# RMSNorm factors applied behind the projections, a router in token rows, and unread products during routing

## The chip, the cores and the metric

The program runs on one core of a Trainium2 chip. The metric is the device time in microseconds (us) of one execution. TensorE is called PE in the rows, VectorE DVE, ScalarE ACT, GpSimd POOL and SyncE SP (SP only issues DMAs here).

## The reference, cut to what matters

Two residual layers over 256 tokens of width 1024, all in float32:

```python
# layer 0
u = rmsnorm(h, ev_norm_mix) @ ev_w_in          # 1024 -> 1952
h = h + attention_a_and_b(u) @ ev_w_out
h = h + swiglu(rmsnorm(h, ev_norm_ff), gate, up, down)          # width 2752
# layer 1
qkv = rmsnorm(h, od_norm_mix) @ od_w_qkv       # 1024 -> 3072
h = h + diff_attention(qkv) @ od_w_out
n = rmsnorm(h, od_norm_ff)
h = h + moe(n, top 2 of 8 by n @ od_router)    # each expert a swiglu of width 3584
```

rmsnorm(x, g) is x * rsqrt(mean(x*x) + eps) * g, by token row. The queries, keys and head outputs have norms of their own, which the change leaves alone.

## The kernel before

**Weights.** They come in units of up to 1 MB (2048 columns on 128 partitions): 66 units for the dense stages, then 42 for each of the 8 experts. SP issues each load into one of RAW = 7 buffers `raw` (four of them in the first stages). ACT rounds a unit to fp32r (`w_hi`, lines 611 and 824), DVE subtracts for the rest (`w_lo`, lines 947 and 1322), and each product of float32 operands is three fp32r matmuls (`product`, lines 1533 to 1535). There are SPLIT = 3 buffers of `w_hi` and `w_lo`, so unit n+3 can be split only when TensorE has used unit n (`unit_used`). Semaphores `hi_ready`, `lo_ready` and `unit_used` count the units. Every engine runs its own program in the order written; a wait holds all that is behind it on that engine.

**Norms.** There are four, k = 0 to 3: ahead of the first input projection, of the dense SwiGLU, of the q/k/v projection, and of router and experts. TensorE accumulates the last unit ahead of norms 1 to 3 in four PSUM banks; when the whole unit is done DVE adds the banks to `h` (`add_out`, line 1052), ACT squares and sums each token half and takes the root (`norm_roots`, lines 642 and 643), DVE takes the reciprocal and multiplies `h` by it into `xs` (`norm_apply`, lines 969 and 970), TensorE transposes `xs` in 16 blocks (`norm_turn`, line 1541), DVE multiplies by the gain (`scale`, line 954), ACT rounds (`parts`, line 618), DVE subtracts (`low_part`, line 961). The next products want the high and low parts of one quarter at a time (`xT_ready`).

**Start.** SP issues the two halves of x, seven gain DMAs, the first weight unit, ten more gain DMAs (`head_gains`), then further units. ACT issues nine small row DMAs (`load_rows`) behind its third split; DVE waits for them, builds eight bias tables (line 1103), and only then splits unit 3. The output of the first 512 columns is copied, squared and normed by DVE and ACT (lines 1107 to 1114), and TensorE turns it (line 1572) behind the second 512 columns.

**Routing.** Logits come as 24 fp32r matmuls with experts as rows, are copied and turned back by TensorE, and DVE picks the two best in 12 dependent steps (lines 1349 to 1363). TensorE counts ranks with five float32 products (lines 1791 to 1795), DVE makes selection matrices `sel` (line 1412), TensorE gathers tokens with them in four groups of eight matmuls (`gather`, line 1806), and ACT and DVE copy the results out of PSUM (lines 899 and 1481). Then DVE lists the overflow work (`spare_items`, lines 1381 to 1406) and expert 0 begins. Gathered rows come from `xn`, the normed rows, split into `xg_hi` (line 893) and `xg_lo` (line 1336).

## Time and profile before

| what | value |
|---|---|
| time, median of 3 runs | 1520.2 us (1518.89 to 1520.89) |
| time of the profiled execution | 1518.86 us |
| its span, first to last instruction | 1516.7 us |
| busy share of the span: PE, DVE, ACT | 95%, 79%, 63% |
| mean granted TensorE clock | 0.966 |

The profiled execution has 2.2 us around its span, and lies 1.3 us below the median. "Idle before <- X" in a row is the time that the engine stood still ahead of the instruction, and X is what let it go. A matmul record is longer than its spacing (0.39 us against a start every 0.23 us), since matmuls are pipelined: the spacing counts.

### The profile page before, as it was taken

How to read it: one execution, taken by the hardware profiler on the slowest of the kernel's cores; microseconds unless marked ns; L12 is line 12 of the kernel's file. 1: busy time of each engine (PE TensorE's matmuls, PEld its weight loads, DVE VectorE, ACT ScalarE, POOL GpSimd, SP SyncE). 2: the span in 40 equal slices, each digit the busy share in tenths (PEclk: the TensorE clock that was granted, in tenths of full speed). 3: DMA queues.
4: the chain of work that ended last, by engine and by line, in shares of the span. 5: the costliest groups of instructions: out<-in, count | busy, mean ns of one | idle time of the engine just before them, and what ended most of it. 6: DMA issues, size and time to landing. Idle time of an engine off the chain costs nothing.

```text
span 1516.7 us, 17820 instructions
## 1 busy us (share of the span) xinstructions
PE 1438.9 (95%) x6619; PEld 1189.3 (78%) x6619; DVE 1191.1 (79%) x1022; ACT 958.9 (63%) x837; POOL 8.4 (1%) x49
## 2 busy tenths in 40 slices
PE   6989899998987699999999999999999999999997
PEld 5768788886866578888888888888888888888886
DVE  7873545445686688899889889888889888888986
ACT  5462534434464367777777777777777777777774
POOL 2000000000000000000000000000000000000000
PEclk9977999999977799999999999999999999999999
DMA  8401755364512269999999999999999998999992
GB/s 278 142 28 51 268 183 192 125 213 142 193 57 85 96 244 375 376 346 375 379 319 377 371 365 359 378 336 344 377 371 347 377 377 311 380 370 354 368 378 112
DMA packets 181295, 421.52 MB, mean 278 GB/s; under 512 B 9192, under 2 KB 12316, under 8 KB 181212
## 3 DMA queue, kind: packets, MB, share of 16 engines
q1 hardware_dynamic: 178172, 418.56, 77.0%
q0 software_dynamic: 560, 1.59, 0.3%
q8 instruction: 57, 0.93, 0.2%
q10 hardware_dynamic: 2480, 0.22, 0.1%
q14 instruction: 26, 0.21, 0.0%
HBM read 419.28 MB, written 1.06 MB: 277 GB/s over the span
## 4 chain that ended last, share of the span: by engine, by line
PE 86%; DVE 9%; ACT 2%; issue 2%; DMA 0%; SPq 0%; DVEq 0%; ACTq 0%
PE ps L1533 26%; PE ps L1535 26%; PE ps L1534 26%; PE ps L1839 2%; DVE w_lo L947 2%; DVE w_lo L1322 1%; PE ps L1806 1%; ACT w_hi L611 1%; DVE h L1434 1%; DVE work L1027 1%; PE ps L1596 1%; PE ps L1541 1%; PE ps L1816 0%; PE ps L1589 0%; PE ps L1612 0%
## 5 line engine op out<-in xcount | busy, mean ns | idle before, releaser
L1322 DVE TENSOR_TENSOR w_lo<-raw,w_hi 128x2048 fp32r<-128x2048 f32 x336 | 768.8, 2290 | 110.3 <-ACT w_hi L824 109.4
L824 ACT ACTIVATE w_hi<-raw 128x2048 fp32r<-128x2048 f32 x336 | 644.2, 1919 | 244.0 <-PE ps L1535 244.0
L1533 PE MATMUL ps<-w_hi,xT_hi 128*128 128x512 f32 (+2 forms) x1312 | 516.5, 394 | 9.4 <-issue 5.3
L1535 PE MATMUL ps<-w_hi,xT_lo 128*128 128x512 f32 (+2 forms) x1312 | 509.0, 388 | 0.0
L1534 PE MATMUL ps<-w_lo,xT_hi 128*128 128x512 f32 (+2 forms) x1312 | 508.7, 388 | 0.0
L1533 PEld LDWEIGHTS ps<-w_hi,xT_hi 128*128 128x128 f32 x1312 | 248.0, 189 | 61.4 <-issue 9.6
L1535 PEld LDWEIGHTS ps<-w_hi,xT_lo 128*128 128x128 f32 x1312 | 247.9, 189 | 51.3
L1534 PEld LDWEIGHTS ps<-w_lo,xT_hi 128*128 128x128 f32 x1312 | 248.4, 189 | 47.8
L947 DVE TENSOR_TENSOR w_lo<-raw,w_hi 128x2048 fp32r<-128x2048 f32 (+4 forms) x66 | 140.6, 2141 | 113.4 <-ACT w_hi L611 113.2
L1533 PE MATMUL ps<-w_hi,hT_hi 128*128 128x512 f32 (+1 forms) x548 | 214.7, 392 | 3.0 <-DVE hT_lo L961 2.0
L1535 PE MATMUL ps<-w_hi,hT_lo 128*128 128x512 f32 (+1 forms) x548 | 213.8, 390 | 0.0
L1534 PE MATMUL ps<-w_lo,hT_hi 128*128 128x512 f32 (+1 forms) x548 | 213.5, 390 | 0.0
L611 ACT ACTIVATE w_hi<-raw 128x2048 fp32r<-128x2048 f32 (+4 forms) x66 | 117.5, 1793 | 135.4 <-PE ps L1535 134.9
L1533 PEld LDWEIGHTS ps<-w_hi,hT_hi 128*128 128x128 f32 (+1 forms) x548 | 103.5, 189 | 24.5 <-DVE hT_lo L961 2.2
L1535 PEld LDWEIGHTS ps<-w_hi,hT_lo 128*128 128x128 f32 (+1 forms) x548 | 103.3, 189 | 21.6
L1534 PEld LDWEIGHTS ps<-w_lo,hT_hi 128*128 128x128 f32 (+1 forms) x548 | 103.4, 189 | 20.7
L849 ACT ACTIVATE hT_hi<-ps 128x512 fp32r<-128x512 f32 x56 | 33.1, 592 | 9.8 <-PE ps L1839 9.8
L1440 DVE TENSOR_TENSOR hT_lo<-ps,hT_hi 128x512 fp32r<-128x512 f32 x56 | 38.3, 684 | 1.3 <-ACT hT_hi L849 1.3
L1456 DVE TENSOR_TENSOR prod_e<-sil_e,ps 128x512 f32<-128x512 f32 x56 | 38.1, 680 | 0.0
L1839 PEld LDWEIGHTS ps<-ident,prod_e 128*128 128x128 f32 x224 | 27.1, 139 | 11.7 <-DVE h L1434 2.9
L1839 PE MATMUL ps<-ident,prod_e 128*128 128x128 f32 x224 | 33.8, 273 | 2.5 <-DVE h L1434 2.5
L874 ACT ACTIVATE sil_e<-ps 128x512 f32<-128x512 f32 x56 | 32.3, 577 | 0.0
(254 smaller groups left out, 739.8 us busy)
## 6 DMA issues: line engine op xcount, KB each, us to landing
raw<-in_od_ex_gate_dram SPq DMA_DIRECT2D x112, 1024.0 KB, 5.8
raw<-in_od_ex_up_dram SPq DMA_DIRECT2D x112, 1024.0 KB, 6.0
raw<-in_od_ex_down_dram SPq DMA_DIRECT2D x112, 1024.0 KB, 5.7
raw<-in_od_w_qkv_dram SPq DMA_DIRECT2D x12, 1024.0 KB, 5.3
raw<-in_ev_ff_gate_dram SPq DMA_DIRECT2D x10, 1024.0 KB, 5.3
raw<-in_ev_ff_up_dram SPq DMA_DIRECT2D x10, 1024.0 KB, 5.3
raw<-in_ev_ff_down_dram SPq DMA_DIRECT2D x10, 1024.0 KB, 4.9
raw<-in_ev_w_in_dram SPq DMA_DIRECT2D x6, 1024.0 KB, 5.6
```

The costliest lines, as they stand in the source:

```text
L611: ins = act.activation(w_hi[0:r, n % SPLIT, a:a + m], raw[0:r, raw_of(n), a:a + m], ACT.Copy)
L824: act.activation(w_hi[:, (DENSE + q) % SPLIT, :], raw[:, r, :], ACT.Copy).then_inc(hi_ready, 1)
L849: act.activation(hT_hi[:, :, side(m)], blocks(4 + m % 2), ACT.Copy).then_inc(hT_part, 1)
L874: act.activation(sil_e[:, j % 2, :], ps[:, 2 * (j % 2), :], ACT.Silu).then_inc(silu_done, 1)
L947: ins = dve.tensor_tensor(w_lo[0:r, n % SPLIT, a:a + m], raw[0:r, raw_of(n), a:a + m], w_hi[0:r, n % SPLIT, a:a + m].bitcast(F32), ALU.sub ...
L1322: dve.tensor_tensor(w_lo[:, k, :], raw[:, raw_of(DENSE + q), :], w_hi[:, k, :].bitcast(F32), ALU.subtract).then_inc(lo_ready, 1)
L1440: dve.tensor_tensor(hT_lo[:, :, side(m)], blocks(4 + m % 2), hT_hi[:, :, side(m)].bitcast(F32), ALU.subtract).then_inc(hT_ready, 1)
L1456: dve.tensor_tensor(prod_e[:, j % 2, :], sil_e[:, j % 2, :], ps[:, 2 * (j % 2) + 1, :], ALU.mult).then_inc(prod_done, 1)
L1533: pe.matmul(out, x_hi, hi, start=start, stop=False)
L1534: pe.matmul(out, x_hi, lo, start=False, stop=False)
L1535: return pe.matmul(out, x_lo, hi, start=False, stop=stop)
L1839: ins = pe.transpose(ps[:, 4 + j % 2, n * P:(n + 1) * P], prod_e[:, j % 2, n * P:(n + 1) * P], ident[:, :])
```

## The change

- **Norm factors.** `h` itself is transposed and multiplied by the gain; the factor 1/rms is applied per token row to what comes out: in the copy of the projections out of PSUM, in the Silu and in the product with it (`rstd` as a per-partition scale). `norm_turn`, `scale`, `parts` and `low_part` no longer wait for roots.
- **Quarters.** `last_unit` orders the last unit by quarters of h (token half, column half), signals each by `out_psum`, and puts the transposes of quarter 0 ahead of the products of the last quarter. DVE adds each quarter by itself (`add_quarter`, `add_and_norm`).
- **Start.** The first two weight units are asked for right behind x; all gain DMAs but one follow them, that one is issued by ACT. Unit 0 is split in halves. DVE's angle steps (lines 1063 to 1080) and ACT's squares come behind the split of unit 1, `load_rows` stays behind the split of unit 2, and `turn_gains` (formerly ahead of the first product) and `router_g` come ahead of the bias tables.
- **Router.** 16 float32 products with tokens as rows, from unnormed `h` and a router multiplied by the gain (the choice of a row does not depend on its factor). No copy and turn of logits; a top search has one step less. Ranks are four products. `xg_hi` and `xg_lo` are made from `hg` = h * gain with the factor in them. `low_tokens(0)` comes ahead of the ranks, `low_tokens(1)` behind `sel`; the split of expert unit 2 and the gate arithmetic (`gates`) move behind the gathered copies, ahead of `spare_items`.
- **Unread products.** `keep_busy` issues 5 fp32r matmuls of 512 columns behind the router and 3 behind the ranks, into a bank that nobody reads.
- **Expert pairs** wait for the first half of the gathered tokens at their first unit and for the second half at their second.

The core of the diff ("..." for what is left out):

```diff
+            def other_gains():
...
-                if n == 1:
-                    head_gains()
+                if n == 2:
+                    other_gains()
...
+            act.wait_ge(gain_ones, 1)
+            act.dma_start(gain_rows[G_MIX0:G_MIX0 + DC, :], w["ev_norm_mix"][0].rearrange("(k p) -> k p", p=P)).then_inc(mix_landed, 16)
...
+                    if n == 0:
+                        act.activation(w_hi[:, 0, 0:UNIT // 2], raw[:, 0, 0:UNIT // 2], ACT.Copy).then_inc(first_hi, 1)
+                        act.activation(w_hi[:, 0, UNIT // 2:UNIT], raw[:, 0, UNIT // 2:UNIT], ACT.Copy).then_inc(hi_ready, 1)
+                        continue
...
+            def norm_square(k, t):
+                if k == 0:
+                    act.wait_ge(x_landed[t], 16)
+                else:
+                    act.wait_ge(h_ready, 4 * (k - 1) + 3 + t)
+                act.activation(squares_3[t] if k == 3 else xs[:, t, :], h[:, t, :], ACT.Square,
+                               accum_out=ssq[:, 2 * k + t:2 * k + t + 1]).then_inc(act_chain, 1)
+                chain[0] += 1
...
+                act.wait_ge(act_chain, chain[0])
+                act.activation(root[:, 2 * k:2 * k + TT], ssq[:, 2 * k:2 * k + TT], ACT.Sqrt,
+                               scale=1.0 / D, bias=eps[:, 0:1]).then_inc(root_ready, 1)
...
+            load_root_table()
+            norm_part(0, 0)
+            split_to(1)
+            for f in range(1, 4):
+                norm_part(0, f)
+            split_to(2)
+            for t in range(TT):
+                norm_square(0, t)
             norm_roots(0)
...
+            def copy_turned(f):
+                t, half = quarter(f)
+                act.wait_ge(xT_psum, 12 + f + 1)
+                act.activation(hT[:, 4 * half:4 * half + 4, t * P:(t + 1) * P], blocks(f), ACT.Copy).then_inc(hT_copied, 1)
+            copy_turned(0)
+            norm_square(3, 0)
+            for f in range(1, 4):
+                copy_turned(f)
+            norm_square(3, 1)
             norm_roots(3)
+            act.wait_ge(rstd_ready, 4)
+            for t in range(TT):
+                act.wait_ge(hg_ready, t + 1)
+                act.activation(xg_hi[:, t, :], hg[:, t, :], ACT.Copy, scale=rstd[:, 6 + t:7 + t]).then_inc(xg_hi_ready, 1)
             split_unit(0, SPLIT - 1)
-            norm_parts(3, 14)
-            for t in range(TT):
-                act.wait_ge(xn_ready, t + 1)
-                act.activation(xg_hi[:, t, :], xn[:, t, :], ACT.Copy).then_inc(xg_hi_ready, 1)
-            act.wait_ge(gate_diff, 1)
-            act.activation(gate_s[:, 5, :], gate_s[:, 4, :], ACT.Exp).then_inc(gate_exp, 1)
...
+            act.wait_ge(gate_diff, 1)
+            for t in range(TT):
+                ins = act.activation(gate_s[:, 5, t:t + 1], gate_s[:, 4, t:t + 1], ACT.Exp, scale=rstd[:, 6 + t:7 + t])
+            ins.then_inc(gate_exp, 1)
...
+            def add_and_norm(stage, last, k, first, c):
+                for f in range(3):
+                    add_quarter(stage, f, last)
+                norm_scale(k, first, c, 0)
+                add_quarter(stage, 3, last)
+                norm_low(c, 0)
+                norm_scale(k, first, c, 1)
+                norm_scale(k, first, c, 2)
+                norm_low(c, 1)
+                norm_scale(k, first, c, 3)
+                norm_low(c, 2)
+                norm_low(c, 3)
+                norm_reciprocals(k)
...
+            norm_scale(0, G_MIX0, 0, 0)
+            norm_scale(0, G_MIX0, 0, 1)
+            norm_low(0, 0)
+            split_to(1)
+            norm_low(0, 1)
+            norm_scale(0, G_MIX0, 0, 2)
+            norm_scale(0, G_MIX0, 0, 3)
+            norm_low(0, 2)
+            norm_low(0, 3)
+            split_to(2)
...
-            dve.wait_ge(router_split, 1)
-            dve.tensor_tensor(router_lo[:, :, :], router[:, :, :], router_hi[:, :, :].bitcast(F32), ALU.subtract).then_inc(router_split, 1)
+            turn_gains()
+            dve.wait_ge(gains_ready, 2)
+            dve.tensor_tensor(router_g[:, :, :], router[:, :, :], gains(G_FF1, DC, E), ALU.mult).then_inc(router_ready, 1)
...
+                dve.tensor_tensor(hg[:, t, :], h[:, t, :], gain_ff[:, :], ALU.mult).then_inc(hg_ready, 1)
+            norm_reciprocals(3)
+            dve.wait_ge(hg_ready, TT)
+            dve.wait_ge(rstd_ready, 4)
...
+            raw_logits = ps[:, 4:6, 0:E]
+            dve.tensor_copy(g[:, 0, :, :], raw_logits)
             def top(src, m, key, hot):
-                link(dve.tensor_reduce(gs[:, m, :], g[:, src, :, :], AX.X, ALU.max))
-                link(dve.tensor_tensor(g[:, key, :, :], g[:, src, :, :], per_token(gs[:, m, :]), ALU.is_equal))
-                link(dve.tensor_tensor(g[:, key, :, :], g[:, key, :, :], keys, ALU.mult))
+                link(dve.tensor_reduce(gs[:, m, :], src, AX.X, ALU.max))
+                for t in range(TT):
+                    ins = dve.scalar_tensor_tensor(out=g[:, key, t, :], in0=src[:, t, :], scalar=gs[:, m, t:t + 1], in1=load8[:, 8, :],
+                                                   op0=ALU.is_equal, op1=ALU.mult)
+                link(ins)
...
+            low_tokens(0)
...
             select(0, 0)
             select(1, 1).then_inc(sel_ready, 1)
+            low_tokens(1)
             for half in range(2):
                 dve.wait_ge(gather_psum, 2 * half + 2)
                 bank = FIRST_BANK[2 * half + 1]
                 dve.tensor_copy(xT_lo[:, 4 * half:4 * half + 4, :],
                                 ps[:, bank:bank + 2, :].rearrange("p b (c n) -> p (b c) n", n=T)).then_inc(x_lo_ready, 1)
+            split_unit(0, SPLIT - 1)
+            gates()
+            dve.wait_ge(rank_psum, 2)
             spare_items()
             dve.wait_ge(routed, 1)
...
+            def last_unit(stage, k, rows, x_hi, x_lo, hi, lo, stop):
+                for f in range(4):
+                    t, half = quarter(f)
+                    tok, col = slice(t * P, (t + 1) * P), slice(half * N, (half + 1) * N)
+                    for c, r in enumerate(rows):
+                        ins = product(ps[:, 4 + TT * t + half, :], x_hi[0:r, c, tok], x_lo[0:r, c, tok], hi[0:r, c, col], lo[0:r, c, col],
+                                      False, c == len(rows) - 1)
+                    ins.then_inc(out_psum if f < 3 else unit_used, 1)
+                    if f == 2:
+                        norm_turn(k, 0)
+                for f in range(1, 4):
+                    norm_turn(k, f)
...
+            def keep_busy(count):
+                for n in range(count):
+                    pe.matmul(ps[:, 0, :], xT_hi[:, n % DC, 0:P], xT_hi[:, 0:2, :].rearrange("p c n -> p (c n)"), start=True, stop=True)
+            pe.wait_ge(router_ready, 1)
+            for f in range(4):
+                t, half = quarter(f)
+                pe.wait_ge(hT_copied, f + 1)
+                for c in range(4 * half, 4 * half + 4):
+                    ins = pe.matmul(ps[:, 4 + t, 0:E], hT[:, c, t * P:(t + 1) * P], router_g[:, c, :], start=(c == 0), stop=(c == DC - 1))
             ins.then_inc(logits_psum, 1)
...
+            keep_busy(5)
             pe.wait_ge(chosen_ready, 1)
...
+            pe.matmul(ps[:, 6, 0:TT * E], tri[:, :], chosen.rearrange("p t e -> p (t e)"), start=True, stop=False)
+            pe.matmul(ps[:, 6, E:2 * E], ones[:, :], chosen[:, 0, :], start=False, stop=True).then_inc(rank_psum, 1)
+            pe.matmul(ps[:, 7, 0:E], ones[:, :], chosen[:, 0, :], start=True, stop=False)
+            pe.matmul(ps[:, 7, 0:E], ones[:, :], chosen[:, 1, :], start=False, stop=True).then_inc(rank_psum, 1)
+            keep_busy(3)
```

## Rows read from the trace of the kernel before

**Rows 1.** The page: the chain that ended last, by engine

```profile
PE 86%; DVE 9%; ACT 2%; issue 2%; DMA 0%; SPq 0%; DVEq 0%; ACTq 0%
```

**Rows 2.** Timeline of all engines, 0 to 42 us (start, length, instruction)

```profile
4.05 0.41 SPq L512 DMA_DIRECT2D raw<-in_ev_w_in_dram  x1
...
9.51 1.91 ACT L611 ACTIVATE w_hi<-raw 128x2048 fp32r<-128x2048 f32 x1 [0.50 <-DMA raw<-in_ev_w_in_dram]
...
16.25 0.77 PE L1533 MATMUL ps<-w_hi,xT_hi 128*128 128x512 f32 x1 [0.78 <-DVE xT_lo L961]
```

**Rows 3.** Busy time in two stretches (last columns: clock, share of 16 DMA engines, GB/s)

```profile
4.00:4.50 0.50, 0.00 (x0) 0.00 (x0) 0.00 (x0) 0.00 (x0) 0.00 (x0) 1.00 0.70 186
...
8.00:8.50 0.50, 0.00 (x0) 0.00 (x0) 0.43 (x3) 0.50 (x1) 0.00 (x0) 1.00 1.03 394
```

**Rows 4.** Timeline of ACT, then DVE, behind the first products

```profile
18.34 0.36 ACTq L595 DMA_DIRECT2D ga_rot<-in_ev_a_qnorm_dram  x1
...
25.84 0.36 DVE L1094 TENSOR_TENSOR lamv<-lamv 128x64 f32<-128x64 f32 x2 [0.56 <-DMA router<-in_od_router_dram]
...
29.54 3.96 DVE L947 TENSOR_TENSOR w_lo<-raw,w_hi 128x2048 fp32r<-128x2048 f32 x2
...
40.38 1.02 DVE L954 TENSOR_TENSOR work<-ps,gcol 128x384 f32<-128x384 f32 x2 [1.78 <-PE ps L1572]
```

**Rows 5.** Timeline of DVE, then PE, around norm 1

```profile
156.67 2.48 DVE L1052 TENSOR_TENSOR h<-h,ps 128x512 f32<-128x512 f32 x4 [1.14 <-PE ps L1535]
...
164.02 0.47 PE L1533 MATMUL ps<-w_hi,xT_hi 128*128 128x512 f32 x1 [0.20 <-DVE xT_lo L961]
```

**Rows 6.** Instructions of one shape, all of them (count | busy us, mean ns)

```profile
L961 DVE TENSOR_TENSOR xT_lo<-work,xT_hi 128x512 fp32r<-128x512 f32 x16 | 11.0, 687 | 1.0 <-ACT xT_hi L618 0.8
```

**Rows 7.** Timeline of DVE, then PE, around norm 2

```profile
355.11 2.48 DVE L1052 TENSOR_TENSOR h<-h,ps 128x512 f32<-128x512 f32 x4 [0.26 <-PE ps L1535]
...
362.54 0.77 PE L1533 MATMUL ps<-w_hi,xT_hi 128*128 128x512 f32 x1
...
364.76 0.39 PE L1535 MATMUL ps<-w_hi,xT_lo 128*128 128x512 f32 x1
```

**Rows 8.** Timeline of DVE, then PE, norm 3 and routing

```profile
501.12 2.48 DVE L1052 TENSOR_TENSOR h<-h,ps 128x512 f32<-128x512 f32 x4 [1.14 <-PE ps L1535]
...
519.99 0.17 DVE L1349 COPY gate_t<-ps 128x16 f32<-128x16 f32 x1 [0.47 <-PE ps L1786]
...
522.48 0.17 DVE L1363 TENSOR_TENSOR gate_t<-gate_t 128x16 f32<-128x16 f32 x1
...
525.32 0.88 DVE L1412 TENSOR_SCALAR sel<-slots_f,rank 128x128 fp32r<-128x128 f32 x4
...
483.82 0.93 PE L1624 MATMUL ps<-ident,xs 128*128 128x128 f32 x7
...
524.43 0.57 PE L1795 MATMUL ps<-gate_t,ones 128*128 128x8 f32 x2
526.25 2.08 PE L1806 MATMUL ps<-sel,xg_hi 128*128 128x256 f32 x8 [1.24 <-DVE sel L1412]
...
534.20 0.47 PE L1533 MATMUL ps<-w_hi,xT_hi 128*128 128x512 f32 x1 [1.36 <-issue]
```

**Rows 9.** Timeline of DVE, then ACT, first units of expert 0

```profile
532.87 1.22 DVE L1481 CAST xT_lo<-ps 128x1024 fp32r<-128x1024 f32 x1 [1.58 <-PE ps L1806]
534.01 0.15 DVE L1381 TENSOR_SCALAR load<-ps 128x8 f32<-128x8 f32 x1
...
539.32 2.29 DVE L1322 TENSOR_TENSOR w_lo<-raw,w_hi 128x2048 fp32r<-128x2048 f32 x1 [0.46 <-ACT w_hi L824]
...
540.02 1.92 ACT L824 ACTIVATE w_hi<-raw 128x2048 fp32r<-128x2048 f32 x1 [0.80 <-PE ps L1535]
```

**Rows 10.** Busy time and granted clock (third column from the end) in stretches

```profile
44.00:45.00 1.00, 1.00 (x5) 0.85 (x4) 0.42 (x2) 1.00 (x2) 0.00 (x0) 0.50 0.00 0
...
98.50:132.00 33.50, 32.04 (x129) 27.06 (x129) 15.63 (x40) 14.15 (x42) 0.00 (x0) 0.50 0.10 32
```

267 lines of the change are left out of this document (139 added, 128 removed).

## Prediction

> **What bounds the kernel now.** I read the page's chain first: TensorE holds 86% of it, DVE 9%, ACT 2% [rows 1]. So the chain is TensorE's products, and what can be won or lost lies where it leaves TensorE. Its pieces in order of time leave TensorE at the start (first product at 16.25), at the four norms, in both attentions, and in routing. The attentions are untouched and only shift. I then read a timeline of each engine at each changed place. All times are in the profiled execution (1518.86 us); it lies 1.3 below the median, and I add that at the end. T below is the time at which DVE's additions to h begin, which is when the last unit's results are there.
>
> **Start.** The first unit is asked for at 4.05 and is there at 9.5; then 1.9 for its rounding, 2.3 for its subtraction, and norm work, until 16.25 [rows 2]. Asked for at about 1.8, it has only x ahead of it. At 8 us the DMA engines are full at 394 GB/s [rows 3]; x and this unit are 2.1 MB, or 5.3 us at that rate from about 3, so I take 8.4 for the landing (8 to 9.4). Halving lets rounding and subtraction overlap: 1.0 + 1.2 + 1.2 gives 11.9, which is the first product, 4.3 earlier.
>
> Most of this is not kept. Behind the split of unit 1 (DVE until 18.8) come ACT's squares and root, then ACT's nine row DMAs. ACT: split of unit 1 until 16.5, two squares 2.3, so that its row DMAs start at 19.05 in place of 18.34, and the rows land at 26.5 in place of 25.8 [rows 4]. DVE cannot pass that wait. Behind it stand 0.75 of lambda work, 0.65 of `turn_gains` and router product (0.2 before), the bias tables of 2.8, and the splits of units 3 and 4 of 3.96 [rows 4]; all end 1.15 later than before. Unit 3 is ready at 33.0, while TensorE wants it at 30.9. TensorE then waits again for the normed columns (39.4). Before, DVE waited 1.8 us for TensorE at that place [rows 4]; now TensorE waits for DVE. The chain goes on at 39.9 in place of 40.4: **0.5 us won**. Bounds: 4.3 if DVE holds nothing up, -1.0 if the unit lands at 9.4 and everything behind it shifts.
>
> The engines' share was 0.70 at 4 us, with 186 GB/s [rows 3]; that is the gap which I expect the early request to fill, and the bound of 9.4 is for the case that it doesn't. One rule speaks against the new order: the Trainium skill, "Trainium Kernel Development and Optimization", section Key Constraints, says that DMAs issued from several engines share the same 16 engines, so that spreading them saves only issue time. By that rule the early request gives nothing, and the result would be that of rival B. The trace agrees for the time around 8, not for that around 4.
>
> **Norm 1.** T = 156.67, first product of the next stage 7.35 later [rows 5]. DVE stands idle for 1.14 before T, behind a split that stays where it is, so its quarters are added at T-1.14, -0.52 and +0.10, 0.62 each (four in 2.48 [rows 5]), although TensorE had them up to 4 us earlier. TensorE has the transposes of quarter 0 ahead of its last six products: it waits from T-1.56 to T-0.45, turns four blocks warm at 0.11 (0.93 for seven with the tail [rows 8]), and ends the last quarter at T+1.4. DVE: gain on quarter 0 until +1.4, fourth addition until +2.2, ACT's rounding meanwhile, subtraction (0.69) until +2.9 [rows 6]. The other transposes end at +2.7. First product at +2.95: **4.4 won**. The second quarter is ready at about +4.6 and wanted at +5.7; the third at 7, wanted at 8.4. ACT's squares and roots lie beside the products; the factor is wanted by the Silu only 11 us later. That they cost nothing rests on these 11 us.
>
> **Norm 2.** DVE is idle only 0.26 before T = 355.11, so all is 0.8 later: first product at T+3.75 in place of +7.43. Here the clock was also low at the first products: the sixth began 2.22 after the first, where 1.14 is the full-clock pace [rows 7]. TensorE now never idles over 2 us there, so I give that 1.1 back: **4.8 won**. For each norm the low bound is 2.5 (roots or DVE hold the quarters up once more), the high one 5.
>
> **Norm 3 and routing.** T = 501.12 [rows 8]. As for norm 1, the last transposes end at T+2.7. ACT copies the four turned quarters and squares between them; they are there in time. The router is 16 float32 products; a float32 product of 8 columns is two records, 0.21 each at the low clock (five products, ten records, from 522.71 to 524.86 [rows 8]), 0.11 at the full one: 3.5 to 6.9 us. I take 4.0: ends at +6.7, in place of +14.4. Choice: 12 steps took 2.66 from the copy at 519.99 [rows 8]; one fewer with three cheap unlinked ones, 2.3: +9.0. Then 0.35 and `low_tokens(0)` 1.25, which now stands ahead of the rank addition, 0.2, and the selection 0.88 [rows 8]: +11.7. TensorE has three unread products behind the ranks; at the low clock these run to +12.0. The gather took 6.8 us for 32 matmuls, all at the low clock until its end [rows 8]. At the full clock it takes 3.5, at the low one 6.8.
>
> **The clock.** TensorE idled from 40.35 to 42.68, and at 44 it is at half (1.2 GHz), although it works again [rows 10]; during routing it was at half from 518 to 532. In the new order it still idles for 1 to 2 us between router, choice, ranks and gather. Eight unread products are 1.8 us of work at full clock. I do not think that this is enough: it falls during router or choice and rises some 4.6 us after the gather has begun (it rose 3.7 us after the first product at 16.25, and 5.8 us after the gather had begun at 526.25). So gather at half until +16.6, the rest at full: first expert product at +17.7 = 518.8 in place of 534.2: **15.4 won** (18.0 if the clock stays full, 14.2 if it stays low through the gather).
>
> **First units of expert 0.** Before, `spare_items` began at 534.01, 0.2 before the first product, and DVE had the split of unit 3 done at 541.6, while TensorE wanted it at 542.7 (unit 1 done at 540.0, 2.7 a unit) [rows 9]. Now the expert begins when the first half has been copied. With E for its first product DVE has: second copy until E+1.3, split of unit 2 2.3 (moved here), gates 1.15 (moved here), `spare_items` 4.85 (534.01 to 538.86), split of unit 3 2.3: E+11.9. TensorE wants it at E+8.5: **a stall of 3.4**. Idling so long, TensorE falls to half, for about 4 us of products: **2.0 lost** (0 to 3.4). Behind it DVE has two units in hand at once and keeps up (2.29 a unit against 2.72).
>
> Other edits at nothing: factor in copies and Silu (same passes over the same tile), the three-operand product (0.06 more on 12 tiles, not waited for), waits of the later expert pairs (no idle there in the waits view), ranks by four products instead of five.
>
> **Sum:** 0.5 + 4.4 + 4.8 + 15.4 - 3.4 - 2.0 = 19.7. 1518.86 - 19.7 = 1499.2; with the 1.3 to the median, 1500.5.
>
> **Rivals.**
> A. The whole start is kept: 3.8 more, 1496.7. For it: DVE's chain may get its rows earlier. Against: rows wait behind ACT's squares. 0.10.
> B. The first unit lands no earlier: 1.5 less, 1502. For it: full DMA engines. 0.12.
> C. The unread products do keep the clock full, in routing and over the stall: 2.6 + 2.0 more, 1495.9. For it: the idle stretches get much shorter than the 3.7 us ahead of the turned logits. Against: 2.3 us of idling at 40.35 was enough for a fall. 0.13.
> D. The quarters are worth half: DVE is late at each norm, and transposes and products of the last unit wait for it: 2.2 less at each of three, 1507. 0.10.
> E. DVE stays behind in expert 0 and a second stall of some 3.4 follows: 1504. For it: DVE is the second busiest engine there. Against: 0.4 us of slack in each unit. 0.10.
> F. Slower: the clock, once down at the stall, stays down. It has done so from 98.5 to 132 with TensorE busy nearly throughout [rows 10]. A product at half takes 0.43 in place of 0.23, so each us of it loses 0.47, and it decides from 42 us on; 60 us would lose 28, for 1529. Against: at each dense stage it rose within 6 us of the first product. 0.03.
> G. No change, because losses elsewhere just cancel the gain: 0.02.
> The forecast has the remaining 0.40, in a range of its own of 1496 to 1505.
>
> A measurement of this kernel tells 0.2%, or 3 us, from no change. Faster: 0.40 + 0.10 + 0.12 + 0.13 + 0.10 + 0.10 = 0.95; same 0.02; slower 0.03. The range of 1493 to 1507.5 leaves out F, G, half of D and some of C with A together (1492).
>
> **What would show it.** First product near 11.9 but the compressed columns turned near 39.9; next-stage products 3 to 4 us after the last unit at norms 1 and 2, and a wait of TensorE of 1 to 2 us for the first addition inside that unit; the choice done near T+9; the gather at about T+12 with a clock of 0.5; first expert product near T+17.7; a wait of TensorE for the split of unit 3 of 3.4 us, its clock at half behind it. The prediction is wrong if DVE's chain at the start takes another way, if the clock stays at 1.0 through routing, or if that wait is missing.

## The result, and the profile after

The changed kernel takes 1507.77 us (median of 7 runs, 1499.01 to 1512.36) against 1520.89 us before; the ratio is 0.9914, 95% interval 0.9889 to 0.9938. That is 13.1 us faster, where 19.7 us were forecast, and 0.3 us above the upper end of the range. The profiled execution lies at the median: span 1505.7 us against 1516.7, so 11.0 us of gain have to be placed. What strikes first is the spread: 13 us in the runs after, under 3 us in the seven before (in the later calls the kernel before spread by 6 to 9 us as well).

The page's chain still belongs to TensorE [rows 1]:

```profile
PE 84%; DVE 10%; ACT 3%; issue 2%; DMA 1%; ACTq 0%; SPq 0%; DVEq 0%
```

Start, timeline of ACT, PE and DVE (answers to [rows 2, 4]):

```profile
10.69 1.06 ACT L621 ACTIVATE w_hi<-raw 128x1024 fp32r<-128x1024 f32 x1 [1.18 <-DMA raw<-in_ev_w_in_dram]
...
14.24 0.77 PE L1628 MATMUL ps<-w_hi,xT_hi 128*128 128x512 f32 x1 [5.29 <-DVE w_lo L999]
...
20.53 0.36 ACTq L607 DMA_DIRECT2D ga_rot<-in_ev_a_qnorm_dram  x1
...
27.70 0.36 DVE L1180 TENSOR_TENSOR lamv<-lamv 128x64 f32<-128x64 f32 x2 [1.62 <-DMA router<-in_od_router_dram]
...
40.63 1.01 DVE L1011 TENSOR_TENSOR work<-ps,gcol 128x384 f32<-128x384 f32 x2
```

The first unit landed later than before (10.7, not 9.5), though it was asked for 2.3 us earlier; from there to the first product it took 3.5 us, as forecast. Behind DVE's chain of rows, tables and splits nothing is left: 40.63 against 40.38.

Norm 1, timeline of DVE and PE (answers to [rows 5]):

```profile
156.57 1.87 DVE L1049 TENSOR_TENSOR h<-h,ps 128x512 f32<-128x512 f32 x3
157.31 0.66 PE L1641 MATMUL ps<-ident,h 128*128 128x128 f32 x4 [0.91 <-DVE h L1049]
...
160.82 0.47 PE L1628 MATMUL ps<-w_hi,xT_hi 128*128 128x512 f32 x1
```

Norm 2, the same (answers to [rows 7]); the first four rows are the end of the feed-forward stage and its last unit:

```profile
344.92 0.41 PE L1856 MATMUL ps<-ident,work 128*128 128x128 f32 x2 [1.13 <-DVE hT_lo L1313]
...
346.37 0.50 PE L1628 MATMUL ps<-w_hi,hT_hi 128*128 128x512 f32 x1 [1.04 <-DVE hT_lo L1313]
...
348.17 0.72 PE L1628 MATMUL ps<-w_hi,hT_hi 128*128 128x512 f32 x1
...
349.68 0.79 PE L1628 MATMUL ps<-w_hi,hT_hi 64*128 64x512 f32 x1
...
358.31 2.82 PE L1641 MATMUL ps<-ident,h 128*128 128x128 f32 x12
...
360.78 0.78 PE L1628 MATMUL ps<-w_hi,xT_hi 128*128 128x512 f32 x1
```

Here the reader is to see the durations: products of 0.63 to 0.79 in place of 0.39 to 0.50, twelve transposes in 2.82 in place of 1.60. The clock was at half from about 348.2 on, 2 us into the last unit, until 362. The busy time by stretch says the same (last three columns: granted clock, share of the DMA engines, GB/s), and shows the first attention at half from 88 us, where before it was 98 us [rows 10]:

```profile
88.00:98.00 10.00, 8.80 (x37) 0.54 0.01 2
98.00:134.00 36.00, 35.33 (x141) 0.51 0.09 30
...
342.00:348.00 6.00, 3.83 (x17) 1.00 0.00 0
348.00:360.00 12.00, 12.00 (x32) 0.51 0.50 175
```

Routing and expert 0 (answers to [rows 8, 9]):

```profile
501.55 3.64 PE L1913 MATMUL ps<-router_g,xs 128*128 128x8 f32 x32
...
507.63 0.18 DVE L1451 TENSOR_TENSOR gate_t<-gate_t 128x16 f32<-128x16 f32 x1
...
511.02 1.91 PE L1934 MATMUL ps<-sel,xg_hi 128*128 128x256 f32 x8
...
516.83 0.40 PE L1628 MATMUL ps<-w_hi,xT_hi 128*128 128x512 f32 x1
...
528.70 0.50 PE L1628 MATMUL ps<-w_hi,xT_hi 128*128 128x512 f32 x1 [3.52 <-DVE w_lo L1404]
```

I divide the span at instructions which both kernels have: the first products behind norms 1, 2 and 3 (the rows above and [rows 5, 7, 8]) and the first output of expert 0, whose place is in the view of the tile `y_lo` (first and last start in us), before and after:

```profile
L1427 DVE TENSOR_TENSOR y_lo<-ps,y_hi x16: 678/682/692, 654.3 to 1507.8; 128x512 fp32r<-128x512 f32 x16
```

```profile
L1518 DVE TENSOR_TENSOR y_lo<-ps,y_hi x16: 679/682/692, 642.3 to 1496.0; 128x512 fp32r<-128x512 f32 x16
```

| us won in the stretch | forecast | profile after | the same kernel again (e1_again) |
|---|---|---|---|
| to the first product behind norm 1 | 0.5 + 4.4 = 4.9 | 164.02 - 160.82 = 3.2 | 4.7 |
| to that behind norm 2 | 4.8 | 1.76 - 3.2 = -1.4 | 2.9 |
| to the first expert product | 15.4 | 17.37 - 1.76 = 15.6 | 19.1 |
| to the first output of expert 0 | -3.4 - 2.0 = -5.4 | 12.0 - 17.4 = -5.4 | -6.3 |
| to the end | 0 | 11.0 - 12.0 = -1.0 | -0.2 |
| sum | 19.7 | 11.0 | 20.2 |

The row of norm 2 needs care: 1.1 of its 4.8 us was to be won behind the first product, by the clock, so that the stretch itself was forecast at 3.7 and the next one at 16.5. A narrower distance shows each place better: from the first product of the last unit ahead of a norm to the first product of the next stage. Before and after it is 13.0 and 8.7 us at norm 1, 13.4 and 14.4 at norm 2, 38.7 and 23.7 at norm 3 with routing.

So norm 1 (4.3), routing (15.0 of 15.4) and the stall are as forecast. Norm 2 is not: it lost 1.0 where 3.7 were forecast. Besides, 1.6 us are missing ahead of norm 1, 0.5 between norms 1 and 2, 0.5 between norms 2 and 3, and 1.0 at the end.

### The profile page after: what moved, and what is told of

It reads as the page before. It is cut to its first block, busy times and chain, and to the rows that moved or that the text cites. A ratio compares the mean times of both kernels' runs of the same rounds, so it can differ in the third digit from the quotient of the medians.

```text
span 1505.7 us, 17825 instructions
## 1 busy us (share of the span) xinstructions
PE 1444.6 (96%) x6632; PEld 1190.9 (79%) x6632; DVE 1180.2 (78%) x1003; ACT 957.8 (64%) x833; POOL 8.4 (1%) x49
## 4 chain that ended last, share of the span: by engine, by line
PE 84%; DVE 10%; ACT 3%; issue 2%; DMA 1%; ACTq 0%; SPq 0%; DVEq 0%
PE ps L1628 25%; PE ps L1630 25%; PE ps L1629 25%; DVE w_lo L1004 2%; PE ps L1967 2%; DVE w_lo L1404 2%; PE ps L1934 1%; DVE h L1525 1%; ACT w_hi L627 1%; PE ps L1711 1%; PE ps L1704 1%; DMA raw<-in_ev_w_in_dram 1%; DVE work L1110 1%; PE ps L1703 1%; PE ps L1641 1%
## 5 line engine op out<-in xcount | busy, mean ns | idle before, releaser
L1630 PEld LDWEIGHTS ps<-w_hi,hT_lo 128*128 128x128 f32 (+1 forms) x548 | 103.7, 189 | 21.9
L1711 PE MATMUL ps<-ident,work 128*128 128x128 f32 x72 | 19.6, 404 | 14.5 <-DVE work L1364 11.4
```

What stands on the lines that cost most here:

```text
L1630: return pe.matmul(out, x_lo, hi, start=False, stop=stop)
L1711: ins = pe.transpose(ps[:, 2 + head % 2, n * P:(n + 1) * P], s[:, slot, n * P:(n + 1) * P], ident[:, :])
```

## Experiments

**The same kernel again, and unread work before norm 2.** Theory: nothing in the order is wrong, but TensorE's clock falls in stretches of which the forecast said that they only shift. Rival: the order of the quarters itself costs time. The first run has no edit; in the second, TensorE has unread products where it waited for DVE twice 1.1 us:

```diff
                             ins.then_inc(ff_turned, 1)
+                            if j == FCH:
+                                for n in range(4):
+                                    pe.matmul(ps[:, (4 * (FCH - 1) + 2) % 3, :], xT_hi[:, n, 0:P], ..., start=True, stop=True)
```

> The changed kernel once more, unaltered. Its own profile gained 4.4 us less than forecast at the second norm (clock at half from 348 us, through the last unit of the feed-forward stage and the transposes) and lost 2.4 us in the first attention (half from 88.7 us in place of 98.5). Theory 1: these are falls of TensorE's clock that strike or miss a place from one execution to the next, because work ahead of them leaves TensorE idle for parts of some us; then the times spread again over some 10 us, the median lies at 1505 to 1510, and this profile shows the fall at another place, or none at the second norm (its first product then 2 to 4 us earlier relative to the additions). Theory 2: the order of instructions causes the loss; then the first product of the next stage comes 8 to 9 us behind the first addition again, with the clock low at the same place, and the times agree within 3 us.

> Eight unread products, four behind each of the last two pairs of transposes of the feed-forward stage, where TensorE waited 1.1 us twice (344.0 and 345.3). They take 0.9 us each time and lie inside the wait. Theory 1 (the clock falls at 348 because of these waits): clock full through the last unit and the transposes of norm 2; 24 products at 0.23 in place of 0.43 and four groups of transposes: 4.5 to 6 us faster than the changed kernel where it had the fall, so a median of 1502 to 1505, and a narrower spread. Theory 2 (the order of the quarters costs it): no change in the distance from the first addition to the next stage's first product, median as the changed kernel within 2 us.

Measured, e1_again: median 1504.38 (1488.61 to 1511.16), profiled execution 1498.59, span 1496.5. Its first products and the same stretches:

```profile
159.36 0.47 PE L1628 MATMUL ps<-w_hi,xT_hi 128*128 128x512 f32 x1
...
344.87 0.50 PE L1628 MATMUL ps<-w_hi,hT_hi 128*128 128x512 f32 x1 [1.04 <-DVE hT_lo L1313]
...
354.99 0.47 PE L1628 MATMUL ps<-w_hi,xT_hi 128*128 128x512 f32 x1
...
507.52 0.40 PE L1628 MATMUL ps<-w_hi,xT_hi 128*128 128x512 f32 x1
```

```profile
88.00:98.00 10.00, 7.74 (x58) 1.00 0.01 2
98.00:134.00 36.00, 34.54 (x137) 0.50 0.09 30
...
342.00:348.00 6.00, 3.84 (x16) 1.00 0.00 0
348.00:360.00 12.00, 11.01 (x53) 1.00 0.50 175
```

The instructions are the same. The last unit began 1.5 us earlier here, so I compare the 6 us ahead of it: TensorE was busy for 3.84 us from 338.87 to 344.87 here and for 3.83 us from 340.37 to 346.37 in the profile after. The clock then stayed at 1.00 here and fell to half there. Behind the fall in the attention TensorE sets the pace, 3.58 us a head:

```profile
98.44 0.79 PE L1703 MATMUL ps<-raw 64*128 64x128 f32 x2
...
102.02 0.79 PE L1703 MATMUL ps<-raw 64*128 64x128 f32 x2
```

From the first product of the last feed-forward unit to the first of the next stage it took 10.1 us here, 14.4 in the profile after, 13.4 before (349.09 to 362.54). Every profile of this order with full clock at that place agrees with the 10.1 (e2_fill, e10 and e15 below). This execution gained 20.2 us. That it is so near 19.7 is partly luck: norm 2 with full clock gave less than forecast, while the stretch behind it gave 19.1 in place of 16.5, with the clock at half for 23.5 us in the second attention (30.5 before) and back earlier in the gather. So theory 1 holds, and the 13 runs of the two calls say how wide it is: 1488.6 to 1512.4 us, mean granted clocks 0.980 to 0.960, about 1.2 us for each 0.001.

e2_fill: 1503.16 (1498.57 to 1508.54); clock full at norm 2 in its profile, 10.1 us from first product to first product. The median is in the forecast range, but its distance to e1_again (1.2 us) is within the spread; what it does to the fall is counted below over all profiles.

**Spare items spread.** `spare_items` becomes a generator, one step of which runs behind each split of expert 0.

```diff
-            spare_items()
-            expert(0, 0, False, False)
+            steps = spare_items()
+            next(steps)
+            expert(0, 0, False, False, steps)
...
                     if q + SPLIT < len(EXPERT):
                         split_unit(i, q + SPLIT)
+                    if q >= 2:
+                        next(iter(steps), None)
```

> The DVE work on spare items (4.85 us in a row before the split of unit 3 of expert 0) is given out one step behind each unit's split in expert 0; nothing is left out. Theory 1 (the stall is this work ahead of a split, and the low clock from 529 to 532.5 is its consequence): the wait of 3.5 us for the split of unit 3 and 1.6 us of low clock are gone, 4.5 to 5.5 us faster than the changed kernel. Theory 2 (DVE has no room: 88.5% busy in steady expert work, and it only falls behind later): waits of 2 to 4 us in all show up at later units of expert 0, and 0 to 2 us are won.

Measured: 1508.46 (1496.9 to 1510.35), nothing won in the median. Yet the wait for unit 3 is gone from its waits view, and from the first expert product to the first output of expert 0 it took 120.4 us, against 125.5 and 126.4 in the two profiles of the changed kernel. Another took its place 480 us later, at the jump back of the loop over expert pairs:

```profile
1001.74 4.69 DVE L1404 TENSOR_TENSOR w_lo<-raw,w_hi 128x2048 fp32r<-128x2048 f32 x2 [4.38 <-ACT w_hi L861]
...
1004.09 0.73 PE L1637 MATMUL ps<-w_hi,xT_hi 128*128 128x512 f32 x1 [2.52 <-DVE w_lo L1404]
```

ACT had ended that `w_hi` at 998.0, so it is not what DVE waited for. The DMA view of 990 to 1006 us has a queue of instruction loads here that it lacks in e1_again:

```profile
q14 instruction: 3, 0.02, 0.4%
```

From the first to the last output it took 856.7 us in place of 853.7 and 853.4. So the stall's gain was partly eaten here, not absent; e12 and e15 take this up.

**The second unit later.** 

```diff
-                if n == 2:
+                if n == 1:
                     other_gains()
```

> The second unit of weights is asked for behind the small gain rows in place of ahead of them; the first unit still right behind x. Theory 1 (the first unit landed at 10.7 and not at 8.4 because the second, asked for 0.4 us behind it, took half of the DMA engines): it lands at 8.4 to 9.4 and the first product comes at 12.2 to 13.0 in place of 14.2; the time hardly changes (0 to 1 us), because DVE's chain behind the row DMAs sets the end of the stage at 40.6. Theory 2 (x and the small tables are what delays it, as the rule of shared DMA engines would have it for any order): it lands at 10 or later still.

Measured: 1507.33 (1488.72 to 1508.68); the first unit's rounding began at 9.69, the first product at 13.24. The unaltered order gave 10.69 and 9.85 in two executions, 13.40 for the product in the second. The effect is at most some tenths: the second unit does not explain the late landing. Theory 1 missed (8.4 to 9.4, product at 12.2 to 13.0); 9.69 is also below the 10 of theory 2. That x and the tables delay it is left, but not shown by itself.

**Unread transposes in the first attention.** `unread_turns(bank)` is eight transposes of the identity into that bank.

```diff
+            pe.wait_ge(q_turned, 3)
+            unread_turns(0)
             pe.wait_ge(qk_normed, 2)
...
+            pe.wait_ge(q_turned, 5)
+            unread_turns(0)
             pe.wait_ge(q_turned, 6)
...
+                if i in (5, 6, 9, 12):
+                    pe.wait_ge(scores_read, i + 2 - len(SCORE_BANKS))
+                    unread_turns(score_bank(i + 1))
```

> 48 unread transposes in the first attention, eight at each of six places where TensorE waited 1.0 to 1.5 us (before the second set of turned heads, before the first scores, before the turned weights of heads 2, 3, 6 and 9). In both profiles of the changed kernel the clock fell at 89 or 98 us and stayed at half until 133 or 136, although from there on TensorE was busy nearly without a gap, at 3.58 us a head in place of some 1.8. Theory 1 (idle stretches ahead of the fall cause it): no fall in this attention, and the 37 to 44 us at half become 20 or so: 12 to 18 us faster than the changed kernel, median 1490 to 1495. Theory 2 (the clock falls for a load that the idle stretches have no part in, so that more work does not help): the fall stays, and the unread work costs 0 to 5 us: 1508 to 1513.

Measured: 1490.91 (four executions, 1489.08 to 1491.1). The clock in the same stretches:

```profile
88.00:98.00 10.00, 9.65 (x71) 1.00 0.00 0
98.00:134.00 36.00, 33.52 (x206) 1.00 0.19 62
```

Theory 1, and the largest effect of the study: 48 transposes that nobody reads give 13 to 17 us. The range of these four runs is 2 us; the six of e1_again have 23. At norm 2 this profile still fell, from 331.5 to 345 us.

**Routing without unread products.** 

```diff
-            keep_busy(5)
...
-            keep_busy(3)
```

> The eight unread products of routing left out; all that is read is computed. Theory 1 (they are too few to hold the clock, as forecast): the clock is at half in the gather with or without them, and the time is that of the changed kernel within 2 us. Theory 2 (they hold the clock through the choice in some executions): 3 to 6 us slower, with half clock from router to gather in the profile. Theory 3 (they stand ahead of the gather and delay it): 0.5 to 1.5 us faster.

Measured: 1508.19 (1501.05 to 1511.91), theory 1. The clock in the stretch between router and gather's end, without them and with them (the profile after):

```profile
508.00:519.00 11.00, 7.70 (x38) 0.53 0.00 0
```

```profile
505.00:516.00 11.00, 10.46 (x44) 0.53 0.00 0
```

TensorE is busier by 2.8 us and the clock is the same. In these two profiles they do nothing. Over all profiles the picture is less clear: with the unread products the clock was at half here for 10 to 10.5 us in ten profiles and for 7 us in four (e1_again, e11, e13, e14), and only one profile is without them.

**Rows first.** `load_rows()` stands right behind ACT's three requests at the start.

> ACT asks for its nine rows at the start, in place of behind its squares and root at 20.5. Theory 1 (DVE's chain behind these rows set the end of the start): DVE's idle 1.6 before the rows is gone, and so are 4.5 us in which ACT's queue issues the requests between its roots and its sine: compressed columns scaled at 38 to 39 in place of 40.6, so 1.6 to 2.6 us faster up to there, unless the first unit lands later for them. Theory 2 (the requests delay the first unit of weights, which shares the DMA engines): unit at 11.5 or later, first product at 15 or later, and nothing won at 40.

Measured: 1508.61 (1503.37 to 1511.48). DVE waits for the rows as long as before, although they were asked for 17 to 18 us earlier:

```profile
27.05 0.36 DVE L1180 TENSOR_TENSOR lamv<-lamv 128x64 f32<-128x64 f32 x2 [1.69 <-DMA router<-in_od_router_dram]
```

```profile
DMA to landing us min/median/max: 20.0/20.0/20.0
```

The second row is the router's request, 3.4 us in the changed kernel. Neither theory: the first unit came no later (9.99), but the requests took longer, 6.8 to 20.0 us where the changed kernel has 3.3 to 4.3. They were among the weight units (366 GB/s from 16 to 24 us); that this sharing is the cause is argued, not tested. The compressed columns were scaled at 39.98.

**Whole unit in place of quarters.** 

```diff
-                for f in range(4):
-                    for c, r in enumerate(rows):
+                for c, r in enumerate(rows):
+                    for f in range(4):
...
-                    dve.wait_ge(out_psum, 3 * stage + f + 1)
...
+                dve.wait_ge(unit_used, last + 1)
```

> The quarters of h are undone alone: the last unit's products run rows by rows as before the change, all four quarters are added when the whole unit is there, and the transposes of quarter 0 stand behind it; factors behind the projections, router and start stay as changed. By the prediction's terms (first product at T+2.95 with quarters, T+7.35 before) the quarters account for about half of it: theory 1: 1.5 to 2.5 us slower at each of three norms, 5 to 7 us in all at the same clock. Theory 2 (the quarters are worth little, since DVE is held up by its split and the products of the last unit wait for the transposes): 0 to 2 us in all. In a single execution a fall of the clock can cover either.

Measured: 1504.63 (1486.3 to 1506.27). Medians cannot tell it here, but the distance from the last unit's first product to the next stage's first product can, since it does not hang on what the clock did elsewhere. At norm 1:

```profile
136.83 0.39 PE L1625 MATMUL ps<-w_hi,xT_hi 128*128 128x512 f32 x1
...
146.56 0.47 PE L1625 MATMUL ps<-w_hi,xT_hi 128*128 128x512 f32 x1 [0.30 <-DVE xT_lo L1018]
```

9.7 us, against 8.7 after (152.15 to 160.82) and 13.0 before (151.03 to 164.02). At norm 2 it is 10.1 (332.08 to 342.20) with quarters or without; at norm 3 23.9 against 23.7. So of the 4.3 us won at norm 1 the quarters give 1.1, the rest, 3.3, stays with the factor behind the projections. At norm 2 the 0 is a difference of two effects: e11 below shows what the order of the quarters costs there. In all 1.3 us, theory 2.

**Both kernels with the unread work.** The kernel before and the changed one, each with the edits of e2_fill and e5_fill_att.

> The kernel before the change, with the unread work of the runs e2_fill and e5_fill_att in the same places: 48 transposes in the first attention, 8 products in the last pairs of transposes of the feed-forward stage. Both this and e10 have no fall of the clock in the first attention, if theory 1 is right, so that their difference is what the change is worth by its own steps. Theory 1 (the forecast's steps were right and falls of the clock in the untouched stretches hid part of them): 1503 to 1507 here, and 16 to 20 us above e10. Theory 2 (the change is worth only the 13 us that the medians showed): 10 to 14 us above e10.

> The changed kernel with both sets of unread work. Theory 1 (both falls come from idle stretches): none in the first attention, none at the second norm; 3 to 5 us below e5_fill_att, which still fell there (331.5 to 345.2): 1485 to 1488, spread under 4 us. Theory 2 (the fall at the second norm comes anyway once the first is gone): 1490 to 1491.

Measured: 1509.31 (1506.23 to 1512.79) and 1484.89 (1483.67 to 1489.63). First products behind the norms: 149.10, 347.58, 519.30 and 143.61, 339.27, 493.43; first output of expert 0 at 639.3 and 618.7. Up to there the change gives 5.5 + 2.8 + 17.6 - 5.3 = 20.6 us, which speaks for theory 1. The first attention has no fall on either side. At the norms the falls are not equal: e9 has them at 145.0 to 148.5 and 343 to 350 us, each behind the wait of 3.87 us that the change removes, and e10 has none there. e10 lies a little below its forecast and spreads by 6 us, not under 4. e9 lies above its own (1503 to 1507), and the medians are 24.4 apart, more than either theory said: the kernel before with the unread work has a wait of its own in the expert loop,

```profile
1011.55 0.80 PE L1533 MATMUL ps<-w_hi,xT_hi 128*128 128x512 f32 x1 [3.45 <-issue]
```

at the same jump back, with the clock at half from 1008.6 to 1015.4. From its first to its last output it takes 859.7 us, where e10 takes 853.4: 6.3 us in all.

**Rows outside, quarters of the last rows.** The loops of e8 again, but each quarter is still announced when its last product is done.

```diff
-                for f in range(4):
-                    for c, r in enumerate(rows):
+                for c, r in enumerate(rows):
+                    for f in range(4):
                         ins = product(...)
+                        if c == len(rows) - 1:
+                            ins.then_inc(out_psum if f < 3 else unit_used, 1)
...
```

> As e10, with the last units' products in another order: all four quarters over the first rows, then quarter by quarter over the last rows. In the changed kernel the last feed-forward unit goes from 128 to 64 rows and back in every quarter, and each product after such a step began 0.36 us late, so that 24 products took 8.26 us in place of 6.81 at the first norm; e8_whole_unit had 10.12 from the 24th last product to the next stage's first at this norm, as the changed kernel with its clock full, and 9.72 against 8.66 at the first. Theory 1 (the steps between rows cost what the quarters give there): 1 us faster at the second norm, 0 to 0.5 at the others, so 1 to 2 us below e10. Theory 2 (later quarters cost what fewer steps give): no difference.

Measured: 1483.88 (1481.58 to 1488.67). The step to another number of rows, in e10:

```profile
330.91 0.19 PEld L1628 LDWEIGHTS ps<-w_hi,hT_hi 128*128 128x128 f32 x1 [0.36 <-issue]
331.80 0.18 PEld L1628 LDWEIGHTS ps<-w_hi,hT_hi 64*128 64x128 f32 x1 [0.36 <-issue]
```

The 0.36 is the idle time of the weight load, not the cost. A product of three matmuls began every 0.89 us behind such steps and every 0.69 without (e11, 329.79 to 330.48), so a step costs 0.2 us.

From first to first product norm 2 takes 9.8 in place of 10.1 us, norm 1 8.5 in place of 8.7. Fewer steps help by 0.2 to 0.4 us where 1 was expected; six steps less are worth 1.2 us, and quarter 0 is announced later. Norm 3 with routing took 21.9 in place of 23.7, but there the clock came back earlier in the gather (488 in place of 491.5 us), which e1_again had without this order. The medians (1.0 apart) agree with either theory.

**Spare items spread, code elsewhere; and the same without the empty instructions.**

```diff
+            for n in range(48):
+                dve.engine_nop()
             dve.wait_ge(rel_landed, 16)
```

> As e10, with the spare items given out step by step as in e3_items and 48 empty instructions at DVE's start, while it waits for its first table. In e3_items the wait for unit 3 was gone, but at the jump back of the loop over expert pairs (999 us) DVE stood idle for 4.4 us with two instruction loads in the records (999.7 and 1002.5) that the changed kernel lacks there. Theory 1 (where the loop's code lies decides whether it is loaded again): with another place no loads at the jump, and 4.5 to 5.5 us below e10, 1480 to 1483. Theory 2 (spreading the items or its new timing causes the wait at the jump, wherever the code lies): the wait stays, and 0 to 2 us are won.

> e12 without the 48 empty instructions, the loop's code where e3_items had it. Theory 1 (its place in the code decides): DVE idle 4 us at the jump back near 980 to 1000 us with instruction loads there, TensorE waiting 2.5 us behind it, and 3.5 to 5 us slower than e12, about what the unread work alone gives (1484 to 1486). Theory 2 (e3_items met it by chance of one execution, or the median of e3_items hid a gain behind falls of the clock): as e12, 1479 to 1481.

Measured: 1479.25 (1477.07 to 1482.91) and 1483.8 (1479.66 to 1488.14), against 1484.89 of e10. e12 has no such wait; e15 has it again:

```profile
981.76 2.29 DVE L1404 TENSOR_TENSOR w_lo<-raw,w_hi 128x2048 fp32r<-128x2048 f32 x1 [4.31 <-ACT w_hi L861]
```

with three instruction loads at 979.7 to 984.9. The two differ in 48 empty instructions that run at the start. The wait is there in both profiles with spread items and without them (e3, e15) and in none of the three with them (e12, e13, e14). So where DVE's code lies decides, though by distances it costs 3.3 us (856.8 from first to last output, 853.5 in e12) where the medians say 4.6. The stall at unit 3 with its half clock is worth 5.6 us by the medians of e10 and e12, and 5.0 by the distance from first expert product to first output (125.3 and 120.3); the forecast was 5.4.

**All together, and wide products inside the router.**

```diff
                 pe.wait_ge(hT_copied, f + 1)
+                keep_busy(2)
```

> The unread work of e10, the order of e11, and the spare items and empty instructions of e12 together. If their gains are separate (e11 1.0 below e10, e12 5.6 below e10, medians): 1477 to 1480. If the clock's falls at the second norm decide (e12's profiled execution had one at 335 us, e10's and e11's had none), medians of such kernels differ by up to 3 us for that alone: 1476 to 1482.

> As e13, with two more unread products of 512 columns ahead of each of the router's four groups of 8-column products, 1.8 us in all at full clock, on the path. Theory 1 (the clock falls for the narrow products, not for waits): clock full until the ranks, or through the gather, whose 32 matmuls then take 3.5 us and not 5 to 6.8: 1.5 to 3 us won against 1.8 lost, so within 1.5 us of e13, and less time at half between 475 and 500. Theory 2 (nothing there depends on the width): clock as in e13 and 1.8 us slower.

Measured: e13 1481.67 (1476.3 to 1482.36), e14 1480.5 (1479.51 to 1485.65). The clock from 486 to 494 us is 0.57 in both, from 478 to 486 it is 1.00 in both; the unread products neither hold it nor show that the narrow ones let it fall. Why it falls in routing stays open. e13 lies above the 1477 to 1480 of gains that simply add up; its profile has a fall at norm 2 (336.5), as its second expectation allowed. The versions with spread items and moved code lie at 1479 to 1482, some 40 us below the kernel before (e12: ratio 0.9723, 0.9702 to 0.9743), 23 to 28 below the changed one. e14 needs 24.5 us from the last unit's first product to the first expert product where e13 needs 21.9; the medians do not show it.

**The falls, counted over all profiles.** First attention: without the 48 transposes the clock fell in 8 of 9 profiled executions (88.4 to 98.5 us, up to 133 to 141), with them in 0 of 8. The ninth is e8_whole_unit, whose profiled execution took 1486.3 us. Last feed-forward unit or norm 2: in the changed kernel and its variants without the eight products 6 of 8, with them 2 of 7 (e12 and e13, at 335 and 337). The first is shown; the second is a tendency. It cannot be the two waits alone: the kernel before was busy for the same 3.84 of 6 us ahead of this unit and kept its clock until its own wait of 3.87 us.

The new order has a share of its own that e1_again did not bring out. In e12, e13 and e4 the clock fell at the first transposes, right behind the wait for the first addition, which only the new order has inside the unit:

```profile
335.20 1.12 PE L1652 MATMUL ps<-ident,h 128*128 128x128 f32 x4 [0.97 <-DVE h L1049]
```

No run fills that wait. Nor does any run fill the second attention, where the clock was at half for 23 to 31 us between 416 and 481 in every profile.

## Why the prediction was wrong

**The step that failed** is in the terms of the clock. At norm 2 the prediction said that TensorE "now never idles over 2 us there, so I give that 1.1 back". It looked at the idle time behind the unit, not at the two waits of 1.1 us ahead of it, nor at the wait of 1 us inside it that it had itself foreseen. In 6 of the 8 profiles of the changed kernel and its variants without the eight products the clock fell there, mostly within 2 us of the unit's start; most of that unit, the transposes and the first products then ran at half. In the profile after, the norm lost 1.0 us in place of winning 3.7, and behind it the clock gave 0.5 of the 1.1. The same mistake stands at its beginning: "The attentions are untouched and only shift." Shifting was enough: in the profile after the fall came at 88.7 in place of 98.5, and the last unit of the stage began at 152.15 in place of 151.03, 0.9 worse than the start alone made it, and over the 13 executions the same kernel differs by 24 us. Since the second call's median (1504.4) lies inside the range, it is chance on which side of 1507.5 a median of this kernel comes out; the missing term is not.

**A size at norm 2, apart from the clock.** With full clock the norm gives 3.3 us (13.4 to 10.1) where 3.7 was forecast. The last unit has 128 and 64 rows in turn, and each step between them costs 0.2 us; before, all products of one row count stood together, so the trace had one such step where the new order has seven. With one step again (e11) the norm gives 13.4 - 9.8 = 3.7, the forecast.

**Factor in the Silu** (0, "same passes over the same tile"). It was not nothing: ACT's pass with the factor takes 0.09 us longer, and TensorE waits for it (first wait 1.26 before and 1.35 after, last 1.00 and 1.09). From the first product behind norm 1 to the last unit ahead of norm 2 it took 185.1 us in both profiles of the kernel before and 185.5 in all 15 of the changed one and its variants, so 0.5 us.

```profile
L770 ACT ACTIVATE work<-ps x12: 322/592/601, 178.5 to 330.9; 128x512 f32<-128x512 f32 x10, 128x192 f32<-128x192 f32 x2
```

```profile
L801 ACT ACTIVATE work<-ps,rstd x12: 412/680/687, 175.3 to 328.2; 128x512 f32<-128x512 f32 x10, 128x192 f32<-128x192 f32 x2
```

**Norm 1** (4.4): 13.0 to 8.7 is 4.3. The mechanism was misread all the same: e8 shows that the quarters are a quarter of it. Rival D priced their failure at 2.2 us a norm; they are worth 1.1, 0 and 0.2.

**Start** (0.5): -0.25 and, in e1_again, 0.4. The chain of DVE did what was said; the landing at 8.4 was wrong, 9.7 to 10.8 in all orders tried, later than the bound of 9.4. Rival B's condition held. The early request gave nothing, as the prediction had read out of the rule quoted against it (the Trainium skill, "Trainium Kernel Development and Optimization", Key Constraints). The rule itself, which is about issuing from several engines, is not tested: SP asks for that unit in both kernels. Another page of the Trainium skill, "DMA: Bandwidth & Descriptors", section Queues, rings and completion order, has each DMA engine take turns between queues a packet at a time; the 20.0 us of e7's 32 KB router request among 1 MB units do not contradict that, and no run tests it.

**Routing** (15.4): 38.7 to 23.7 is 15.0 (15.1 between e9 and e10); choice done at 507.8, gather at 511.0, its clock 0.5, all as forecast. **Stall** (3.4): 3.52. **Clock behind it** (2.0): 5.4 for both together. **Rival C**: its condition did not hold, the clock fell in routing in every profile. e6 shows no effect of the unread products where they stand, though the idea works elsewhere (e5). **Rivals E and F** did not occur; G neither.

**To the end** (0): -1.0. From first to last output the profiles take 853.5 and 853.7 us; 0.8 us come behind SP's request for the output (1510.78 of 1516.7, 1498.97 of 1505.7), in the transfer, which the change does not touch.

Put together: the change gives about the forecast 19.7 us when the first attention's fall is the same on both sides and norm 2 has none in the changed kernel (20.2 in e1_again, 20.6 up to the first output with unread work on both sides). The median over the 13 executions is 13 us, because this kernel meets the second fall more often than not. The range was built from places of the trace and had no term for that; of the 13 executions 4 lie in it.

## What to carry to other kernels

Ask of each stretch at full clock how near it is to a fall, also of those that the edit only shifts: list TensorE's waits ahead of every dense run, and fill them with unread work in a bank that is free anyway, before counting microseconds at the norms. Compare two kernels by distances between the same instructions with the clock of each stretch beside them, and profile the same kernel twice before explaining a difference of 10 us. When a removed stall does not show in the time, look for another at a loop's jump.

## What the runs showed of the hardware

In e1_again TensorE waited five times between 76 and 98 us (1.1, 1.1, 1.5, 1.2 and 1.1 us; one more wait was 0.35), was busy between them, and fell to 1.2 GHz at 98.2. Once down, the attention was bound by TensorE, and the clock stayed down for 38 us (44 in the profile after, where TensorE was busy in 35.3 of 36.0 us). At half, the same work filled the engine and that did not bring it back; filling the waits kept it from falling in all 8 profiles that had the 48 transposes.

At a loop's jump back DVE stood idle for 4.3 us and TensorE for 2.5, with instruction loads in the records, or neither did; 48 instructions of displacement made the difference. A request of 32 KB took 20.0 us to land among full queues, 3.4 otherwise. A step from 128 to 64 rows, or back, leaves TensorE's weight load idle for 0.36 us at full clock and costs 0.2 us. A Silu of 128 x 512 with a factor per row took 0.68 us on ACT, without it 0.59.
